# Expert slices of 80 columns, a table of overflow items and a fifth weight slot in a hybrid decoder step

## The reference, cut to what matters

```python
gl = xf @ w_group + b_group                    # 4 groups
gidx = top_1(gl)                               # one group for each token
ev, eidx = lax.top_k(el_sel, 2)                # two of its 8 experts
ew = softmax(ev) * g_gate
for e in range(32):
    he = jax.nn.silu(xf @ w_exp_gate[e]) * (xf @ w_exp_up[e])
    y = y + combine[:, e:e + 1] * (he @ w_exp_down[e])
```

## Time and profile before

| | us |
|---|---|
| median of 3 runs | 684.52 |
| lowest and highest | 683.84, 686.62 |
| the profiled execution | 683.11 |
| its span, first to last instruction | 681.4 |
| PE busy | 637.1 (93%) |
| DVE busy | 348.0 (51%) |
| ACT busy | 196.0 (29%) |
| POOL busy | 90.0 (13%) |

### The profile page before, as it was taken

One profiled execution on the slowest core, in us unless ns is written; L12 is line 12 of the kernel. 1 busy time (PEld: TensorE's weight loads), 2 busy tenths in 40 slices (PEclk: granted clock), 3 DMA queues, 4 the chain that ended last, 5 costly groups with the idle time before them and its releaser, 6 DMA issues.

```text
span 681.4 us, 18765 instructions
## 1 busy us (share of the span) xinstructions
PE 637.1 (93%) x8135; PEld 569.4 (84%) x8135; DVE 348.0 (51%) x679; ACT 196.0 (29%) x312; POOL 90.0 (13%) x97
## 2 busy tenths in 40 slices
PE   5999999899798989999999789999999999999993
PEld 4577777667698989987688589999999999999982
DVE  2159988889899999662268322121211211112235
ACT  3120012455753446431282301101201110111033
POOL 1011110416297500250000000000000000000000
PEclk8699999899899999999868989999999999999997
DMA  9775164033333334540580009999999999999102
GB/s 263 235 226 193 54 222 148 2 123 124 124 124 124 124 124 153 161 185 1 204 351 1 1 2 366 389 374 404 391 404 387 420 389 396 401 366 422 70 1 69
DMA packets 41751, 145.06 MB, mean 213 GB/s; under 512 B 6958, under 2 KB 10262, under 8 KB 29414
## 3 DMA queue, kind: packets, MB, share of 16 engines
q1 hardware_dynamic: 33424, 140.88, 54.0%
q10 hardware_dynamic: 8294, 3.73, 2.4%
HBM read 143.02 MB, written 2.43 MB: 213 GB/s over the span
## 4 chain that ended last, share of the span: by engine, by line
PE 55%; DVE 7%; issue 2%; ACT 1%; DVEq 0%; ACTq 0%
PE bank L1469 25%; PE bank L1486 12%; PE bank L1366 5%; PE bank L1296 4%; PE bank L1419 3%; PE bank L1523 2%; PE bank L1238 2%; DVE w_lo L935 1%; PE bank L1393 1%; PE bank L1381 1%; PE bank L1507 1%; DVE conv L978 1%; DVE half L1050 1%; ACT work L781 1%; DVE gel_lo L935 0%
## 5 line engine op out<-in xcount | busy, mean ns | idle before, releaser
L1469 PE MATMUL bank<-work,ring 128*64 128x96 f32 x4096 | 177.6, 247 | 5.8 <-DVE work L1178 5.8
L1469 PEld LDWEIGHTS bank<-work,ring 128*64 128x64 f32 x4096 | 174.9, 139 | 5.9 <-issue 5.9
L1301 PE MATMUL bank<-work,ring 128*128 128x304 f32 x512 | 136.2, 427 | 0.9 <-ACT work L535 0.9
L1301 PEld LDWEIGHTS bank<-work,ring 128*128 128x128 f32 x512 | 99.2, 194 | 36.0 <-issue 3.2
L866 DVE SCALAR_TENSOR_TENSOR bank<-work,par,bank 128x272 f32<-128x272 f32 x232 | 96.4, 497 | 0.0
L1486 PE MATMUL bank<-windows,ring 128*64 128x96 f32 x2048 | 91.6, 246 | 0.0
L1197 DVE TENSOR_TENSOR windows<-bank,outst 128x192 f32<-128x192 f32 x32 | 11.4, 357 | 152.7 <-ACT outst L763 152.7
L1486 PEld LDWEIGHTS bank<-windows,ring 128*64 128x64 f32 x2048 | 88.9, 137 | 0.1
L763 ACT ACTIVATE outst<-bank 128x192 f32<-128x192 f32 x32 | 10.6, 330 | 137.2 <-PE bank L1469 137.2
L935 DVE TENSOR_TENSOR w_lo<-ring,w_hi 128x2048 fp32r<-128x2048 f32 x17 | 39.5, 2328 | 15.3 <-ACT w_hi L616 15.3
L1296 PE MATMUL bank<-xn_hi,w_hi 128*128 128x304 f32 x128 | 39.8, 311 | 7.9 <-DVE xn_lo L935 5.0
(11 more groups left out here) (269 smaller groups left out, 820.2 us busy)
## 6 DMA issues: line engine op xcount, KB each, us to landing
ring<-w_exp_gate SPq DMA_DIRECT2D x32, 1024.0 KB, 7.3
ring<-w_exp_up SPq DMA_DIRECT2D x32, 1024.0 KB, 9.5
ring<-w_exp_down SPq DMA_DIRECT2D x32, 1024.0 KB, 11.5
ring<-w_in SPq DMA_DIRECT2D x11, 2048.0 KB, 8.5
ring<-w_rnn_proj SPq DMA_DIRECT2D x2, 2048.0 KB, 7.8
ring<-w_conv_proj SPq DMA_DIRECT2D x2, 2048.0 KB, 8.5
ring<-w_out SPq DMA_DIRECT2D x2, 2048.0 KB, 8.4
ring<-w_in SPq DMA_DIRECT2D x2, 1024.0 KB, 10.7
```

The costliest lines, as they stand in the source:

```text
L1301: ins = mm(bank[m % 4][:, 0:T], mix_w[b % MIX_SLOTS][:, i, (c % MB) * P:(c % MB + 1) * P], xnT[:, i], start=(i == 0), stop=(i == KT - 1))
L1469: ins = mm(bank[s % 2][lo:lo + HP, (2 * m + f) * C:(2 * m + f + 1) * C], w_gu[s][m][:, k, f, lo:lo + HP], xw[s % 2][:, k], start=(k == 0), ...
```

## The change

- **C is 80 instead of 96.** Windows, gate/up, silu, `hid`, down and results all have 80 columns.
- **No passes.** The pass loop is gone on all engines, and with it `npass`, `rbase`, the copy `xn2` of the normed rows (three ScalarE activations) that a second pass would have read, and GpSimd's two memsets of `ys`. An expert's ranks from 80 on go to slots behind all experts' own ones, and DVE writes a table of *overflow items*, each a window of 80 columns of one expert: `over_e` (which expert), `over_at` (where), `over_n` (their number plus one). They are worked off one by one behind the 32 experts, each with a load of its expert's weights. The table is built on DVE right behind the first two windows.
- **A fifth slot.** `EXP_SLOTS` is 5. Its gate matrix lies in a new buffer `extra`, up and down in the part of `work` where `xn2` was. `dynamic_dma_scratch_size` is set to 2048 to make room in SBUF; it concerns DMAs that GpSimd issues, of which there are none. SP loads experts 1, 0, 2, 3, 4 up front.
- **Split waits.** SP waits for `gu_mm` (gate/up done) ahead of gate and up of the next expert in a slot, and for `dn_mm` ahead of its down.
- **The loop.** gate_up(0) stands in front; three iterations of ten experts follow, each gate_up(i) with down(i - 1) behind it; gate_up(31), down(30) and down(31) stand behind the loop.

The core of the diff:

```diff
-C = 96
+C = 80
-EXP_SLOTS = 4
+EXP_SLOTS = 5
+RING_SLOTS = 4
+EXP_LOOP = 10
...
-            def load_expert(e, s):
-
+            def load_expert(e, s, gate_up_used=None, down_used=None):
+
+                if gate_up_used is not None:
+                    sp.wait_ge(gu_mm, gate_up_used)
                 for m, n in enumerate(("w_exp_gate", "w_exp_up")):
                     sp.dma_start(w_gu_flat[s][m], a[n][0, bass.ds(e, 1)].rearrange("e (p k) f -> p (e k f)", p=P))\
                       .then_inc(gu_in[s], 16)
+                if down_used is not None:
+                    sp.wait_ge(dn_mm, down_used)
                 sp.dma_start(w_dn_flat[s], a["w_exp_down"][0, bass.ds(e, 1)].rearrange("e (p k) n -> p (e k n)", p=P))\
                   .then_inc(dn_in[s], 16)
...
-            for e in (0, 2, 3):
+            for e in (0, 2, 3, 4):
                 load_expert(e, e)
...
-            for t in SPLIT_ORDER:
-                n = ROWS[t]
-                nc.scalar.activation(grouped(xn2[0:n, t]), dealt(x[0:n, t]), ACT.Copy,
-                                     scale=stat[0:n, 9 + t:10 + t]).then_inc(xn2_done, 1)
...
+            own, over = cwin[:, 0:NE], cwin[:, NE:]
+            step.beside(vec.tensor_scalar(own, cnt, float(C), None, ALU.min))
+            step(vec.tensor_scalar(over, cnt, float(C), 0.0, ALU.subtract, ALU.max))
+            step(vec.tensor_tensor_scan(off, ones_b[:, 0:2 * NE], cwin, 0.0, ALU.mult, ALU.add))
...
+            step(vec.tensor_tensor(one_of, each(item_no), numbers, ALU.is_equal))
+            step(vec.tensor_tensor(one_of, one_of, each(item_at), ALU.mult))
+            step(vec.tensor_reduce(table_f[:, MAX_OVER:2 * MAX_OVER], one_of, AX_X, ALU.add))
...
+            vec.tensor_copy(over_i, table_f).then_inc(over_done, 1)
...
+            gate_up(0, 0, 0, 32, 1)
+            with pe.Fori(0, (NE - 2) // EXP_LOOP) as g:
+                for s in range(1, EXP_LOOP + 1):
+                    i, loads = g * EXP_LOOP + s, s // EXP_SLOTS + 1
+                    gate_up(i, s % EXP_SLOTS, s % 2, g * (32 * loop_loads) + 32 * loads, i + 1)
+                    if s == 2:
+                        pe.wait_ge(wT_done, 4)
+                    loads = (s - 1) // EXP_SLOTS + 1
+                    down(g * EXP_LOOP + (s - 1), (s - 1) % EXP_SLOTS, (s - 1) % 2, g * (16 * loop_loads) + 16 * loads)
...
+            pe.wait_ge(over_done, 1)
+            items = pe.value_load(over_n, min_val=1, max_val=MAX_OVER + 1)
+            with pe.If(items > 1):
```

More of the change, by code:

```diff
@@ new lines, in _ @@
+            silu(0, 0)
+            with act.Fori(0, (NE - 2) // EXP_LOOP) as g:
+                for s in range(1, EXP_LOOP + 1):
+                    silu(g * EXP_LOOP + s, s % 2)
+                    results(g * EXP_LOOP + (s - 1), (s - 1) % 2, results_at(g * EXP_LOOP + (s - 1)))
+            silu(NE - 1, 1)
+            results(NE - 2, 0, results_at(NE - 2))
+            results(NE - 1, 1, results_at(NE - 1))
+            act.wait_ge(over_done, 1)
+            items = act.value_load(over_n, min_val=1, max_val=MAX_OVER + 1)
@@ new lines, in _ @@
+            with act.If(items > 1):
+                with act.Fori(1, items) as r:
+                    silu(r + (NE - 1), 0)
+                    at = act.value_load(over_at[:, bass.ds(r - 1, 1)], min_val=0, max_val=SLOTS)
+                    results(r + (NE - 1), 0, at)
+            with act.Else():
+                act.nop()
+            act.wait_ge(wT_done, 4)
+            for q in range(2 * PT):
+                j, w = q // 2, min(P, SLOTS - q // 2 * P)
+                act.wait_ge(yT_mm, q + 1)
+                nc.scalar.activation(yrow_hi[0:w, j, q % 2 * 512:(q % 2 + 1) * 512], bank[q % 2][0:w],
+                                     ACT.Copy, scale=wpair[0:w, j:j + 1]).then_inc(yT_act, 1)
@@ new lines, in _ @@
+            hidden(NE - 1, 1)
+            results(NE - 2, 0, offset(NE - 2))
+            results(NE - 1, 1, offset(NE - 1))
+            dve.wait_ge(over_done, 1)
+            items = dve.value_load(over_n, min_val=1, max_val=MAX_OVER + 1)
+            with dve.If(items > 1):
+                with dve.Fori(1, items) as r:
+                    at = dve.value_load(over_at[:, bass.ds(r - 1, 1)], min_val=0, max_val=SLOTS)
+                    window(at, 0)
+                    hidden(r + (NE - 1), 0)
+                    results(r + (NE - 1), 0, at)
@@ new lines, in gather @@
+            def gather(q, t):
+                n = ROWS[t]
+                for part in (xn2_hi, xn2_lo):
+                    ins = mm(bank[q % 4][:, 0:T], part[t][0:n, q // 2 * P:(q // 2 + 1) * P],
+                             sel[0:n, t, (q % 2) * T:(q % 2 + 1) * T],
+                             start=(t == 0 and part is xn2_hi), stop=(t == NT - 1 and part is xn2_lo))
+                return ins
+            for t in range(NT):
+                if t == 0:
+                    pe.wait_ge(hi_done, NT)
+                    pe.wait_ge(lo_done, NT)
+                pe.wait_ge(sel_done, t + 1)
+                for q in range(4):
+                    ins = gather(q, t)
+                    if t == NT - 1:
+                        ins.then_inc(gat_mm, 1)
@@ new lines, in _, with turn @@
+            with pe.Else():
+                pe.nop()
+            keep_clock(0, 7)
+            pe.wait_ge(ys_act, items + (NE - 1 + RESULTS_BEFORE))
+            pe.wait_ge(ys_dve, items + (NE - 1 + RESULTS_BEFORE))
+            def turn(q):
+                if q >= 2:
+                    pe.wait_ge(yT_dve, q - 1)
+                j, w = q // 2, min(P, SLOTS - q // 2 * P)
+                for i in range(4):
+                    ins = tp(bank[q % 2][0:w, i * P:(i + 1) * P], ys[:, 4 * (q % 2) + i, j * P:j * P + w], ident)
+                ins.then_inc(yT_mm, 1)
```

545 lines of the change are left out of this document (249 added, 296 removed).

## The result

The changed kernel takes **712.44 us** (median of 4 runs, 709.31 to 715.42) against 684.35 us of the kernel before on the same chip: ratio 1.040, 95% interval 1.034 to 1.047. The forecast was 651.1 us, 33 us less than before; what came is 28 us more. The profiled execution took 715.42 us, its span 713.3.

A forecast was written before the change was run, and what follows sets the result against it. PE was taken to set the loop's pace, with DMA needing only 7% less. The loop falling from 255.55 to 221.7 us (-33.9) plus 0.5 behind it gave -33.4: 651.1 us against 684.52, range 645.5 to 666.

The forecast's parts named there:

- What bounds the kernel before: Expert loop: PE sets the pace at 7.93 us per expert; DMA alone needs 7.40, only 7% less.
- The record: PE matmul in the expert loop: 80 columns bring it from 41.25 ns to 34.6 ns, 6.64 us per expert.
- Loop of PE alone, 214.3 us: Expert loop without DMA limits: 32 x 6.64 = 212.5 us, plus 1.8 for the start at half clock.
- The DMA chain: Weight loads in the loop: 7.40 us per expert, PE waiting from about expert 25; loop ends at 221.7 us.
- Instruction loading, "I take 3": PE instruction packets in the loop: 1.1 us of DMA time if kept, 3.4 if loaded each pass; 3 taken.
- The rule against the loop of ten: PE has 128 KiB of instruction memory in 16 KiB blocks, so the ten-expert body is fetched anew each pass.
- Rival 1: Unkept body stalls PE at each of two back edges, 2 to 10 us uncovered: 653 to 661 us; chance 0.12.
- Rival 2: Weight loading holds the PE record at 41.25 ns, the loop stays at 255 us: 684 us; chance 0.08.
- Rival 3: Instruction packets all through one DMA engine, 9.2 us per expert in the loop, +8.6: 693 us; chance 0.07.
- Rival 4: Overflow items occur after all, some 15 us each behind the experts: 666 us for one; chance 0.02.
- The back edge, "nothing to gain": Loop of ten takes the back edge 2 times instead of 7; no gap there now, so no gain.
- Behind the loop: PE, ACT and DVE load the number of items and branch: 0.5 us taken, bounds 0 and 1.5.

The follow-up runs named there:

- the body of four: The changed kernel with four weight slots and a loop body of four experts in place of five and ten: 664.07 us, ratio 0.968.
- 80 columns alone: The kernel before with expert slices of 80 columns for 96 and nothing else of the change: 663.27 us, ratio 0.968.
- loads of a sixteenth: The changed kernel with every expert load after the first five cut to 128 of 2048 words per partition row: 657.7 us.
- the body of five: The changed kernel with five experts in the loop body for ten and a third buffer of each kind: 719.92 us, ratio 1.050.
- the body of eight: The changed kernel with four weight slots for five and eight experts in the loop body for ten: 710.83 us, ratio 1.036.
- the body of six: The changed kernel with three weight slots for five and six experts in the loop body for ten: 721.22 us.

## Why the prediction was wrong, step by step

- **What bounds the kernel before: right.** PE set the pace, and the DMA engines needed 7% less time per expert.
- **The record: right.** 34.5 ns measured, 34.6 said.
- **Loop of PE alone, 214.3 us: the record right, the clock mis-sized.** The start at half speed cost 2.4 us (1.8 said). But the clock fell again around stalls, and that took 19 us more, which no term held.
- **The DMA chain: right for a body that is kept, never reached here.** With the body of four the DMA engines are full in the middle of the loop, and from expert 20 on PE runs at their pace, 7.45 us per expert against the 7.40 said, and waits for `w_exp_up`:

```profile
536.68 4.65 PE L1500 MATMUL bank<-work,ring 128*64 128x80 f32 x128 [0.50 <-DMA ring<-w_exp_up]
...
544.13 4.65 PE L1500 MATMUL bank<-work,ring 128*64 128x80 f32 x128 [0.58 <-DMA ring<-w_exp_up]
```

```profile
440.00:600.00 160.00, 154.71 (x4416) 153.24 (x4412) 27.98 (x69) 17.08 (x46) 0.00 (x0) 1.00 1.01 419
395.49:628.69 233.20, 220.19 (x6144) 217.76 (x6144) 45.56 (x113) 23.33 (x63) 0.00 (x0) 0.98 0.92 379
```

  The same working with one slot less gives 221.7 + 7.4 = 229.1 us; measured 233.2, and 236.1 with 80 columns alone. The 4.1 us on top are of the size of the 5.0 us that PE stood in the first pass with the body of four, a stall that I had read off the kernel before as absent. Of the 7.0 with 80 columns alone such stalls are 3.4; the rest no run takes apart.
- **Instruction loading, "I take 3": this is the step that failed.** I had the right packets (45 foreseen for the loop if not kept, 52 counted) and the right share of the engines, and I priced them as load on the DMA engines: 45 x 1.2/16 = 3.4 us. That is what they cost the weights. What they cost PE is the time until they arrive, once in every 256 instructions: 48.6 us of standing and some 19 of half speed. I had taken from the earlier trace rows, five packets in the first pass, and from the loop's PE rows without a stall, that reading ahead hides them. But there PE ran through a block in 5.28 us, no load was issued in the first 15 us of that pass, and all later passes fetched nothing. It was one pass of the easiest case, carried to 52 packets in a harder one.
- **Sum of it:** the loop took 282.5 us and not 221.7, 60.8 more: 48.6 of stalls, 19.6 of half speed (21.4 less the 1.8 that the forecast had), less 7.4 of waiting for weights that no longer came up.
- **The rule against the loop of ten** was weighed and given 0.12. Its first half held: the body was fetched in each pass. Rival 1 made the stall one of the back edge only. The two back edges cost 4.17 and 4.57 us, 8.7 in all, inside its 2 to 10; the 25 stalls in mid-body were in no case. So the rule named the right event, a body that isn't kept, and the forecast of 653 to 661 built on it was still 51 us or more short.
- **Rival 2** (record not set by columns): wrong. **Rival 3** (all packets on one engine): its sign came true, its mechanism not. It needs PE to wait for weights, and PE waited for none in the loop. **Rival 4**: no items.
- **Fifth slot up front, split waits, overflow table, before the loop:** about as said. 80 columns alone and the changed kernel with a body of four, which has all the rest but the fifth slot, give 0.968 and 0.968. The loops of the trial kernels start between 394.1 and 396.5, except one at 401.8, so the 2.4 us at the start are mostly scatter. The back edge, "nothing to gain", was mis-sized with the loading: 8.7 us.
- **Behind the loop: mis-sized.** 2.5 us against 0.5 said, 2.1 of it in two issue waits. The first, 1.17 us ahead of the keep-clock matmuls, stands in every run with the table and not with 80 columns alone; with the DMA engines idle it is no shorter (1.53 with loads of a sixteenth). So it goes with the register load and its branch; whether the load or the fetch behind the branch takes it, no run tells. The second, 0.92, is 0.46 with loads of a sixteenth and gone with the body of four.
- **What I had named as proof of error** was a slow record, early waits for weights, or a slow stream with a full queue. None of them came; the idle time had a releaser that I hadn't listed.

What stays open: where a late block waits. The runs show that it is late in proportion to the weight traffic, not whether it stands behind weight packets in one engine's queue or shares its bandwidth.

## What to carry to other kernels

Count the instructions of a loop's body on the engine that sets the pace: a block of 64 f32 matmuls is 128 records here, each with a weight load of its own, and a body of 105 KiB was kept where one of 113 was fetched again in every pass. Price a fetch by its latency against the time in which the engine runs through 256 instructions, not by its bytes, and expect it late often where the DMA engines are busy. Idle time with the releaser "issue" in the middle of equal instructions, at distances of 256 or a multiple, with packets of q8 beside it, is the sign of it (the word alone is not); the cure is a shorter body, and a spare buffer can still be filled once, outside the loop.

## What the hardware showed that I had not expected

- PE stops at block boundaries while all its operands are there: 25 times, up to 3.5 us, with 52 fetched packets that took just 1.2% of the DMA engines' time.
- An unhidden fetch at a back edge costs 3.1 to 3.3 us with the DMA engines nearly idle. Under the weight loads it took 4.2 to 4.6 in the changed kernel and 5.4 to 6.0 in the body of five, but 3.1 to 3.2 in the body of eight and 2.8 to 4.0 in the body of six. What sets it between 2.8 and 6.0 is open.
- Between a body of 105 and one of 113 KiB the count of packets goes from 30 to 84. Five experts in the body (719.92 us) are no better than ten.
- An instruction of PE that only holds two satisfied waits takes about 105 ns in a long row of them (13.45 us for 128).
